# Modulation chunks moved from the S5 recurrence into the mLSTM stage of a two-block kernel, with states in pairs and the division on ACT

## What is computed

```python
mod = jax.nn.silu(c) @ w_mod[l] + b_mod[l]
mod_c = jax.nn.silu(c_ctx) @ w_mod[l] + b_mod[l]
sh1, sc1, g1, sh2, sc2, g2 = jnp.split(mod[:, None, :], 6, axis=-1)
```

```python
num = einsum('bhts,bhsd->bhtd', s, vc) + w_inter[..., None] * einsum('bhvk,bhtk->bhtv', C, qc)
den = jnp.sum(s, axis=-1) + w_inter * einsum('bhk,bhtk->bht', n, qc)
h = num / jnp.maximum(jnp.abs(den), jnp.exp(-m_t))[..., None]
...
hn = (h - mu) * lax.rsqrt(var + LN_EPS) * norm_w.reshape(MLSTM_HEADS, MLSTM_HD)
```

## Time and profile before

| | us |
|---|---|
| median of 3 runs | 2561.15 (2558.32 to 2562.78) |
| profiled execution | 2560.47, its span 2558.7, mean granted clock 0.95 |
| PE, DVE, ACT busy over the span | 2339.7, 1268.5, 782.0 |
| S5 stage | 381 to 469.5 |
| mLSTM stage | 469.5 to 557.6 |

### The profile page before, as it was taken

One profiled execution on the slowest core, in us unless ns is written; L12 is line 12 of the kernel. 1 busy time (PEld: TensorE's weight loads), 2 busy tenths in 40 slices (PEclk: granted clock), 3 DMA queues, 4 the chain that ended last, 5 costly groups with the idle time before them and its releaser, 6 DMA issues. The chain is left out here.

```text
span 2558.7 us, 26286 instructions
## 1 busy us (share of the span) xinstructions
PE 2339.7 (91%) x10746; PEld 1748.1 (68%) x10746; DVE 1268.5 (50%) x1864; ACT 782.0 (31%) x1237; POOL 140.3 (5%) x128
## 2 busy tenths in 40 slices
PE   6999988779899999999999899978797998886999
PEld 3445753567788878788878589945577875443787
DVE  3779529365644334345533564057553385553311
ACT  3101122433333322244322433234362231344210
POOL 0000000300000000000000000054100000011000
PEclk9999988859999999999999999989898998898999
DMA  7440028023233333234333221000202111001332
GB/s 254 157 130 25 17 67 320 1 93 96 75 99 95 95 99 99 83 92 131 100 96 90 67 61 42 10 1 33 79 25 91 34 41 66 5 14 55 104 94 58
DMA packets 272911, 204.15 MB, mean 80 GB/s; under 512 B 17650, under 2 KB 252458, under 8 KB 271864
## 3 DMA queue, kind: packets, MB, share of 16 engines
q1 hardware_dynamic: 257772, 186.31, 24.1%
q0 software_dynamic: 3136, 10.25, 1.1%
q10 hardware_dynamic: 11884, 5.91, 0.9%
HBM read 175.26 MB, written 26.01 MB: 79 GB/s over the span
## 5 line engine op out<-in xcount | busy, mean ns | idle before, releaser
L1941 PE MATMUL bk_in<-h_part,w_part 128*128 128x512 f32 x2112 | 484.8, 392 | 9.5 <-DVE h_part L2229 6.7
L1941 PEld LDWEIGHTS bk_in<-h_part,w_part 128*128 128x128 f32 x2112 | 398.1, 189 | 95.5 <-DVE h_part L2229 7.1
L2027 ACT ACTIVATE w_part<-w_raw 128x1024 fp32r<-128x1024 f32 (+1 forms) x136 | 154.4, 1136 | 547.8 <-PE bk_in L1941 315.7
L2164 DVE TENSOR_TENSOR w_part<-w_raw,w_part 128x1024 fp32r<-128x1024 f32 (+1 forms) x136 | 179.2, 1318 | 225.6 <-ACT w_part L2027 225.5
L1941 PE MATMUL bk_out<-hid_part,w_part 128*128 128x512 f32 x1056 | 243.8, 393 | 7.6 <-DVE hid_part L2240 7.6
L1941 PEld LDWEIGHTS bk_out<-hid_part,w_part 128*128 128x128 f32 x1056 | 200.4, 190 | 50.8 <-DVE hid_part L2240 8.4
L3640 PE MATMUL fo_ps<-fo_hi,fo_part 128*128 128x512 f32 x512 | 161.3, 394 | 21.0 <-DVE fo_part L2388 20.2
L990 PE MATMUL fr_ps<-arena,work 128*128 128x512 f32 x384 | 168.3, 600 | 5.2 <-DMA work<-in_w_in 5.2
L2501 PE MATMUL bk_in<-h_part,sj_part 128*128 128x512 f32 x576 | 135.6, 396 | 6.5 <-DVE h_part L2252 5.4
L990 PEld LDWEIGHTS fr_ps<-arena,work 128*128 128x128 f32 x384 | 73.5, 192 | 96.4 <-issue 90.5
L2911 PE MATMUL aj_ps<-h_part,aj_part 128*128 128x512 f32 x576 | 137.8, 400 | 0.0
(11 more groups left out here) (560 smaller groups left out, 3332.4 us busy)
## 6 DMA issues: line engine op xcount, KB each, us to landing
w_raw<-in_w_ffn_in SPq DMA_DIRECT2D x88, 512.0 KB, 3.8
work<-in_w_mod SPq DMA_DIRECT2D x24, 1024.0 KB, 8.1
w_raw<-in_w_ffn_out SPq DMA_DIRECT2D x32, 704.0 KB, 4.6
work<-in_w_in SPq DMA_DIRECT2D x25, 512.0 KB, 3.7
w_raw<-in_w_in SPq DMA_DIRECT2D x20, 512.0 KB, 3.8
w_raw<-in_w_out SPq DMA_DIRECT2D x16, 512.0 KB, 4.1
work<-in_w_out SPq DMA_DIRECT2D x8, 1024.0 KB, 6.9
kept_mix<-work SPq DMA_DIRECT2D x12, 512.0 KB, 2.6
```

The costliest lines, as they stand in the source:

```text
L1941: mm = pe.matmul(bank, w_part[:, n % 2, a, k, :], moving(b, k), start=(first and k == 0 and j == 0), stop=(last and k == kt - 1 and j == 2))
L2027: nc.scalar.activation(w_part[:, n % 2, 0, 0:kt, :], w_raw[:, n % 2, 0:kt, :], ACT.Copy)\
L2164: nc.vector.tensor_tensor(w_part[:, n % 2, 1, 0:kt, :], w_raw[:, n % 2, 0:kt, :], f32(w_part[:, n % 2, 0, 0:kt, :]), ALU.subtract).then_in ...
```

## The change

Modulation chunks 10 and 11 (columns of g2; `MOD_L` = 10) are computed in the mLSTM stage, in 8 steps of two products with 512 KB of weights each from a ring of four tiles, between the row products 4 to 7 and behind the last. DVE copies their rows out and adds their bias, ahead of its first score weights; the first `intra` waits for that. The S5 stage has 12 steps left, all among the input products, and reads the spill back behind load 8. State products come two in a turn (0; 1, 2; 3, 4; 5, 6; 7). In the turns the division of pairs 0 to 2 goes to ACT, 16 pieces each, and the steps of a pair stand in successive turns: `invert`, `division` (ACT), `center`, `variance`, `norm`. The first `turn_heads` keeps its place and its wait, while `norm(1)` moves from turn 6 to turn 7. The diff without the placing of buffers and declarations:

```diff
@@ stage_mlstm, PE
+                    else:
+                        pe.wait_ge(m.added, 1)
...
+                def modulation(n):
+                    q = n // 4
+                    pe.wait_ge(loaded[n % 4], 16 * q + 16)
+                    for k in range(2):
+                        kk = 2 * (n % 4) + k
+                        tile = 32 * (kk % 3)
+                        mm = pe.matmul(pI[tile:tile + 2, q, :], S.cs[:, kk, :], ring[n % 4][:, k, :],
+                                       start=(kk < 3), stop=(kk >= KT - 3))
+                    mm.then_inc(m.used, 1)
+                def turn_row(q):
+                    pe.wait_ge(m.pick, 3)
+                    pe.wait_ge(m.rowc, 3 * q + 3)
...
-                for i in range(NT):
...
-                    rows(i)
+                for u in range(2 * HEADS):
+                    if u < 4:
+                        if u:
+                            state(2 * u - 1)
+                        state(2 * u)
+                    if u == 4:
+                        state(NT - 1)
+                    rows(u)
+                    if u >= 4:
+                        modulation(2 * u - 8)
+                        modulation(2 * u - 7)
+                turn_row(0)
...
                     mm.then_inc(s.scores, 1)
+                    if i == 0:
+                        turn_row(1)
                     if i:
                         out(i - 1)
@@ SP
+                for n in range(4 * N_MOD):
+                    if n >= 4:
+                        sp.wait_ge(m.used, n - 3)
+                    k, at = 2 * (n % 4), (MOD_L + n // 4) * HALF
+                    sp.dma_start(ring[n % 4], w_mod[:, k:k + 2, at:at + HALF]).then_inc(loaded[n % 4], 16)
@@ ACT (its state copies in the same pairs)
+                def division(r):
+                    act.wait_ge(s.inverse, r + 1)
+                    for j in range(16):
+                        at = sums[:, 2 * r + j // 8, j % 8 * V1:j % 8 * V1 + HD]
+                        o = nc.scalar.activation(at, at, ACT.Copy, scale=den[:, 16 * r + j:16 * r + j + 1])
+                    o.then_inc(s.divided, 1)
                 for i in range(NT):
                     inter(i)
-                    if i >= 2:
-                        (squares if i % 2 == 0 else root)((i - 2) // 2)
+                    if i >= 2 and i % 2 == 0:
+                        division(i // 2 - 1)
+                    if i >= 3 and i % 2:
+                        squares((i - 3) // 2)
+                    if i >= 4 and i % 2 == 0:
+                        root(i // 2 - 2)
+                root(NT // 2 - 2)
                 squares(NT // 2 - 1)
@@ DVE (three memsets and three small copies ahead of the states)
+                for q in range(N_MOD):
+                    dve.wait_ge(m.used, 4 * q + 4)
+                    for j in range(3):
+                        tile = slice(32 * j, 32 * j + 2)
+                        nc.vector.tensor_copy(rows_of[q][tile, :], pI[tile, q, :]).then_inc(m.rowc, 1)
+                dve.wait_ge(m.turned, N_MOD)
...
-                    if i >= 4 and i % 2 == 0:
-                        norm(i // 2 - 2)
-                    if i >= 2 and i % 2 == 0:
-                        divide(i // 2 - 1)
-                    if i >= 3 and i % 2:
-                        variance(i // 2 - 1)
+                    if i >= 2 and i % 2 == 0:
+                        invert(i // 2 - 1)
+                    if i >= 3 and i % 2:
+                        center((i - 3) // 2)
+                    if i >= 4 and i % 2 == 0:
+                        variance(i // 2 - 2)
+                    if i >= 5 and i % 2:
+                        norm((i - 5) // 2)
+                variance(NT // 2 - 2)
+                combine(NT - 1)
+                invert(NT // 2 - 1)
+                divide(NT // 2 - 1)
                 norm(NT // 2 - 2)
-                combine(NT - 1)
-                divide(NT // 2 - 1)
+                center(NT // 2 - 1)
                 gated(0)
@@ stage_s5
-    N_MOD = MOD_N - MOD_H
+    N_MOD = MOD_L - MOD_H
...
-                for n in range(3, DT):
+                for n in range(3, 2 * N_MOD):
                     load(n)
-                    if n == 10:
+                    if n == 8:
                         sp.dma_start(A.view(V.ca_back, V.N_CA), S.spill[:, 0:V.N_CA]).then_inc(s.back2, 16)
...
-                for n in range(DT - 2):
-                    if n + 4 < DT:
-                        inputs(n + 4)
+                for n in range(2 * N_MOD):
+                    inputs(n + 4)
                     modulation(n)
...
                 outputs(0)
-                modulation(DT - 2)
                 outputs(1)
-                modulation(DT - 1)
```

65 lines of the change are left out of this document (53 added, 12 removed).

## The result

The changed kernel takes **2573.72 us** (median of 4 runs, 2572.36 to 2578.71) against 2560.28 of the kernel before, run beside it: ratio 1.0056, 95% interval 1.0038 to 1.0073. It is slower, and by more than the range allowed. The profiled execution has a span of 2572.1 us. A second series of the same kernel gave 2574.33 (6 runs, 2563.60 to 2577.83; ratio 1.0042, 1.0027 to 1.0057). It spreads over 14 us; what that means is taken up under r1_after.

The account below looks back on a forecast made before the run. Each stage was priced by its last chain, with PE, mostly at 1.2 GHz, bounding the turns. S5 -5.2 and matrix memory +8.7 (3.2 - 1.7 + 4.7 + 2.5) gave 3.5 us longer, 2565 us, range 2556.5 to 2570.5.

Parts of the forecast that it names:

- F: S5 stage: input product behind step 10 late, recurrence ends 3.1 us later, 3.5 more on any case; 2568.5; chance 0.12.
- S5: forecast -5.2: State space stage: fewer modulation steps and a hidden turned row, less a low-clock charge, make it 5.2 us shorter.
- about 3 us at low clock, +1.0: S5 outputs: PE, idle before them, runs about 3 us at low clock, costing 1.0 us.
- The entry: Matrix memory stage up to the first value product: it starts at 504.9 against 501.7, 3.2 us later.
- I take nothing: Entry, latency of loads 4 to 7: nothing if under 3.4 us, some 1.5 if two come late; none charged.
- The first turn: Start of the turns: clock holds only through the first turn's value product, 3.60 to 1.93, saving 1.7 us.
- A: Turns: clock holds through turns 0 to 3, falls at turn 4's stall; 4.6 us less than forecast, 2560; chance 0.27.
- The stall: Last turn: first head transposes wait for norm(1) behind center(2) and ACT's division, starting 4.7 us later.
- The tail: From the last turn's transposes to the stage's end: 19.4 us against 16.9, 2.5 longer.
- D: Entry: clock falls between the paired states, rows and modulation run at 1.2 GHz; 3 us more, 2568; chance 0.20.
- E: Turns: clock holds to the end, through the stall, and the tail runs faster; 2553.5; chance 0.08.
- The sign: Whole kernel against the one before: within 0.2% 0.47, slower 0.40, faster 0.13.

Follow-up runs that it names:

- r1_after: The changed kernel, unchanged, run again as a second series; 2574.33 us, ratio 1.0042 to the kernel before.
- x7: Changed kernel with modulation steps one at a time, the turns as before the change, and unread products in PE's waits and turns; 2562.30 us, ratio 1.0014.
- x10_pool: Changed kernel with one wait constant changed, so POOL prepares a chunk state one ahead; 2570.38 us, ratio 1.0038.
- x11: Changed kernel with the spill read issued behind load 10 instead of load 8; 2568.87 us, ratio 1.0036.
- y2: Kernel before the change with only the new order of the turns, division on ACT; 2568.65 us, ratio 1.0030.
- x14: x8 with unread products only ahead of the turns, none in them; 2553.38 us, ratio 0.9970.
- x4: Changed kernel with unread 128x252 products ahead of each state, around the last row's turning and in each turn; 2581.51 us, ratio 1.0076.
- x9: x8 with unread products ahead of the outputs, in the turns of the exponentials and in the first seven turns; 2555.64 us, ratio 0.9978.
- x13: x9 with the spill read issued behind load 10; 2557.48 us, ratio 0.9988.
- y1: Kernel before the change with unread 128x252 products ahead of the first inter-chunk product and in the first seven turns; 2558.73 us, ratio 0.9993.
- x8: Changed kernel with one modulation step per turn, POOL one state ahead, first row copies earlier, first head transposes behind the last turn's products; 2560.13 us, ratio 0.9992.

## Why the prediction was wrong, step by step

**The bound of each part** was read rightly: the last chains named for both stages are those of the profile after, and the pieces of the table add up to the difference. Two small slips stand in the sums. The terms of the S5 stage add to -5.3, not -5.2. And F is 3.1 us late in the recurrence but adds 3.5 to the time.

**S5: forecast -5.2, measured -2.9.** Outputs, steps 14 and 15 and the hidden row went as said. The term mis-sized is the clock: "about 3 us at low clock, +1.0" was 6 us, and the outputs took 16.48 instead of 13.84 (x7), +2.6. The other 0.58 is rival F in small. Priced at 3.1, it came at nothing (r1_after) to 2.73 us (x10_pool) in the kernels with the spill behind load 8, and it goes with the spill's place (x11).

**The entry: forecast +3.2, measured +7.9.** This is the step that failed. The count of the order was good: it gave 35.35 us from the stage's start (504.9 less 469.55), and r1_after, nearly all at full clock and with the loads nearly in time, has 36.05. The first profile has 4.05 more, in three pieces against r1_after: key transposes at 1.2 GHz (first state 7.13 us after the start instead of 6.01, +1.1), the late load (+1.5; "I take nothing" was the wrong end of the two that stood there), and the clock's fall ahead of the first value product (turned row to value product 5.83 instead of 4.42, +1.4). Only one set of scores and an inter product stand on PE between the second turned row and the value products, but they take 2.03 us at 1.2 GHz and 1.09 at 2.4. So the term that failed is PE's path through the entry, priced at full clock and with no late load.

**The first turn: forecast -1.7, measured 0** in the first profile, and by their times in the seven runs near it. I took the fall to come inside it; it came 3 us earlier. In r1_after it came four turns later. What I left unpriced is that both courses exist in one kernel. I had bound them as cases (A with 0.27) without seeing that the range has to hold both with every other error on top.

**The stall: +4.7, measured +5.3**, place and chain as forecast. The division's 16 pieces took 3.94 us, 0.246 each, not 0.2. The Trainium skill (ScalarE: Activation LUTs, What ACT_TABLE_LOAD costs) has the figures for an estimate of 0.24 for a piece and 3.8 us for the division. The trace agrees, with 3.94 us. The eight pieces of 65 elements in the earlier trace rows, 0.22 each, are a little below it. **The tail: +2.5, measured +1.7.** y2 confirms the sum of both on its own, 7.03 against 7.2.

**Unforeseen**: the semaphore clearing, -0.5 in sum, 0.5 us ahead of the S5 stage and 1.4 us behind the mLSTM stage.

**Rivals.** D (the clock falls between the paired states) did not come: the waits of 1.2 us there left the clock at 1.00. A is the course of r1_after, waits and all: I wrote intra(4) 3 us late, it came 3.7 late. Its total of 2560 was missed by 3.6 us, and that profile has 3.4 us more behind the stage than the kernel before. E came in neither profile. The errors of 1.7 (first turn), 4.7 (entry), 2.3 (S5) and 1.4 (behind) all had one sign. The smaller ones, +0.6 for the stall, +0.5 ahead, -0.8 for the tail and -0.5 for the clearing, nearly cancel, and the sum of 3.5 became 13.4. The sign had been put at slower 0.40; same, at 0.47, was the wrong first choice.

**The clock.** The earlier trace rows have PE busy 43.48 of 43.6 us at 0.52, and I took this for the products' own level. r1_after runs the same loop, PE busy 12.83 of 13 us, at 1.00. So in these profiles the loop, without added products, keeps whichever level it is entered with, until PE waits. The Trainium skill (TensorE: Matmul & The Clock Gate, What's actually happening) says that activity releases the throttle; in the first profile a PE that was busy without a pause for the 33.76 us of the turns was not released, so a busy PE is not enough here. The section also says that one kernel's number of slow products at its start varies from run to run. No run here measures that; but the two profiles of the changed kernel differ likewise, in the level of four turns in the middle.

## What to carry to other kernels

A step that moves into another stage costs what stands behind it in each queue, not its own time. The eight steps, 7.5 us of products that looked hidden, lengthened the entry by some 4 to 7 us. Once they stood one to a turn, with the first copies ahead of the backward pass and POOL one state ahead, the entry was 0.3 us longer than before the change. Before moving work to another engine, look which engine has slack at the clock that the loop really runs at, and what waits at the head of the fast engine's queue. Where a loop can be entered at either clock level, price both courses for every kernel of the comparison and let the range hold both; large products in the waits ahead of it can help to settle which it is (x14), but too many lengthen the path (x4) and late ones come behind the fall (x7).

## What the runs showed of the hardware that was not expected

The same program took two courses in the same stage, 108.4 and 97.1 us. With 128x252 products added in the turns, the clock stayed up through all of them in x4. In x7, x9, x13 and y1 it fell at a wait for DVE of 1.7 to 2.6 us and was back one set of value products later (a wait of 1.91 us in x7 left it up). Without added products in the turns it stayed down after the wait of turn 4 (r1_after, x8, x11, x14). Ahead of the turns it fell in the first profile at 505, where PE had had no wait above 1.52 us since 488, and in x7 at 497.5, behind a wait of 0.97 us and with PE busy without a pause since. Loads of 512 KB on an otherwise idle queue landed in 4.4 us in one run and 5.9 in another. What decides the level in a given execution, and the load's time, stays open.
